# Gate and value products of five dense feed-forward stages with the weights as the stationary operand

## The chip, the core and the metric

The kernel runs as one launch on one core of a Trainium2 chip. The metric is the time on the device in microseconds (us); lower is better. The engines go by their names in the profile: PE is TensorE (its weight loads stand apart, as PEld), DVE is VectorE, ACT is ScalarE, POOL is GpSimd, SP is the engine that issues most transfers.

## What is computed

The reference runs 256 tokens of width 1024 through two blocks of two layers each: mixers (convolution and state space, dilated attention, then retention, gated recurrence and windowed attention) with feed-forward parts between them. Five of these parts are dense, with an inner width of 2816, and the change is about them:

```python
def rms_norm(x, g):
    y = xf * lax.rsqrt(jnp.mean(xf * xf, axis=-1, keepdims=True) + NORM_EPS)
    return (y * g.astype(jnp.float32)).astype(x.dtype)

def swiglu(u, w1, w2):
    gate, up = jnp.split(u @ w1, 2, axis=-1)
    return (jax.nn.silu(gate) * up) @ w2

# first block, in each of two layers, before and after the mixer:
h = h + 0.5 * rms_norm(swiglu(rms_norm(h, g[0]), ffn_w1[i, 0], ffn_w2[i, 0]), g[1])

# second block, layer 0:
ff = (jax.nn.silu(h @ w_gate) * (h @ w_up)) @ w_down
```

In order of time they are called ffn00, ffn01, ffn10, ffn11 (first block) and ff0 (second block). The last feed-forward part, of the second block's layer 1, is a mixture of experts and has code of its own, which the change leaves alone.

## The kernel before, in words

**Three products for one.** A matrix product in float32 is made of three products of a shorter format (float32r in the code, `fp32r` in the profile). Each operand is split into a high part (ACT writes it by a copy) and a low part (DVE subtracts the high part from the original). `products` (L1009) and `turned_products` (L540) issue high by high, high by low and low by high into one bank. In `products` the tokens are the stationary operand, which PEld loads, and 512 columns of weights stream past; in `turned_products` 128 columns of weights are stationary and 256 tokens stream, and the result comes out with the tokens along the free axis. The mixers use both forms, the dense stages only `products`.

**A dense stage** has 11 blocks of 256 inner columns. For each block SP loads 2 MB of gate and value weights and 1 MB of down weights. A block is split as three units: unit 0 (the first four of eight 128-row chunks of the gate and value weights), unit 1 (the other four) and unit 2 (the down weights). `pe_dense` (L1021) has this step:

- `up` of block j+1: for unit 0, then unit 1, for both halves t of the tokens, 4 chunks of 3 products of 512 columns (256 of the gate, 256 of the value) into bank 4 + t: 48 products.
- `down` of block j for the first half of the tokens: 12 products of 512 columns into the banks 0 and 1.
- `turn` of block j+1: four 128x128 transposes of the product of silu and value, so that the inner columns come to stand on the partitions, into bank 6. It waits for `hidden_ready`.
- `down` for the second half of the tokens: 12 products into the banks 2 and 3.

The first block has no `down` ahead of it; the last `down` stands behind the loop. In `act_dense` (L1156) and `dve_dense` (L1187) a step is: split unit 0 of the block after next, silu of the gate half of banks 4 and 5 (L1169, ACT), multiply with the value half (L1199 or L1203, DVE), split unit 1, high part of the turned result (L1177, ACT), low part (L1211, DVE), split unit 2. Each engine works through its list in order.

**The norm.** For the four stages of the first block the input isn't normed: the tokens' scale (`token_scale`, one number per token) is applied behind the product, as the `scale` of the silu and the scalar of DVE's multiply, where the tokens are on the partitions. So the products can start before the sum of squares is known. ff0 has no such scale.

**The start of a stage.** `pe_turn_h` (L1242) turns the hidden state h in four parts of four transposes: parts 0 and 1 are the first half of the tokens, 2 and 3 the second. ACT (L1261) and DVE (L1272) split each into `u_high` and `u_low`. All four stand ahead of the first product on PE. The first half's h comes some 2.7 us ahead of the second half's.

**The end of a stage.** ACT copies the last down unit (L1141), then, in ffn00, ffn10, ffn11 and ff0, splits the first four pieces of the next stage's weights (L407), then loads the table with the square root (L619) and squares the result (L666); DVE follows (L1150, L416, L692, L703) and writes the new h.

## Time and profile before

| what | value |
|---|---|
| time, median of 3 runs | 3358.28 us (3352.33 to 3360.78) |
| the profiled execution: its own time, its span | 3354.18 us, 3352.3 us |
| PE busy | 3183.7 us, 95% of the span |
| DVE, ACT busy | 2259.7 us (67%), 1870.2 us (56%) |
| PE's share of the chain that ended last | 89% |
| granted clock of PE, mean | 0.975 of 2.4 GHz |

The busy time of PE is not a sum of work: a product's record lasts longer than the distance to the next one, since they are pipelined. For what a product costs, the distance from start to start is read. The granted clock has two levels, 0.50 (1.2 GHz) and 1.00 (2.4 GHz).

### The profile page before, as it was taken

How to read it: one execution, taken by the hardware profiler on the slowest of the kernel's cores; microseconds unless marked ns; L12 is line 12 of the kernel's file. 1: busy time of each engine (PE TensorE's matmuls, PEld its weight loads, DVE VectorE, ACT ScalarE, POOL GpSimd, SP SyncE). 2: the span in 40 equal slices, each digit the busy share in tenths (PEclk: the TensorE clock that was granted, in tenths of full speed). 3: DMA queues.
4: the chain of work that ended last, by engine and by line, in shares of the span. 5: the costliest groups of instructions: out<-in, count | busy, mean ns of one | idle time of the engine just before them, and what ended most of it. 6: DMA issues, size and time to landing. Idle time of an engine off the chain costs nothing.

```text
span 3352.3 us, 41787 instructions
## 1 busy us (share of the span) xinstructions
PE 3183.7 (95%) x15980; PEld 2665.0 (79%) x15980; DVE 2259.7 (67%) x2676; ACT 1870.2 (56%) x2461; POOL 14.4 (0%) x26
## 2 busy tenths in 40 slices
PE   6999989999999989999899999997999999999998
PEld 5878578788887877888688788886888888788886
DVE  4549855555445565656554647555998898898997
ACT  4441354544555445646444447463777777777775
POOL 0000000000000000000000000000000000000000
PEclk9999999999999989999899999997999999999999
DMA  8444265555436444534454344434999999999994
GB/s 271 163 157 151 75 201 170 183 191 172 132 101 208 138 176 151 186 132 152 166 195 176 139 151 151 142 122 162 350 365 353 333 366 354 333 366 354 355 355 185
DMA packets 381165, 719.10 MB, mean 215 GB/s; under 512 B 14025, under 2 KB 153743, under 8 KB 380847
## 3 DMA queue, kind: packets, MB, share of 16 engines
q1 hardware_dynamic: 376384, 707.71, 59.6%
q0 software_dynamic: 2368, 8.52, 0.7%
q8 instruction: 123, 2.02, 0.2%
q10 hardware_dynamic: 2223, 0.31, 0.1%
q14 instruction: 67, 0.55, 0.0%
HBM read 715.44 MB, written 1.05 MB: 214 GB/s over the span
## 4 chain that ended last, share of the span: by engine, by line
PE 89%; DVE 5%; ACT 4%; issue 1%; ACTq 0%; DMA 0%; DVEq 0%; SPq 0%
PE duo L1011 13%; PE duo L1012 13%; PE duo L1013 13%; PE acc L1011 8%; PE acc L1013 8%; PE acc L1012 8%; PE aux L1011 2%; PE aux L1013 2%; PE aux L1012 2%; PE duo L387 1%; PE duo L542 1%; PE duo L543 1%; PE duo L544 1%; PE aux L542 1%; PE aux L543 1%; PE aux L544 1%
## 5 line engine op out<-in xcount | busy, mean ns | idle before, releaser
L1583 DVE TENSOR_TENSOR weights_split<-w,weights_split 128x1024 fp32r<-128x1024 f32 x672 | 790.6, 1221 | 107.9 <-ACT weights_split L1562 106.8
L1562 ACT ACTIVATE weights_split<-w 128x1024 fp32r<-128x1024 f32 x672 | 677.6, 1057 | 247.6 <-PE duo L1013 168.1
L1011 PE MATMUL duo<-weights_split,u_high 128*128 128x512 f32 x1776 | 699.7, 394 | 10.7 <-issue 5.8
L1013 PE MATMUL duo<-weights_split,u_low 128*128 128x512 f32 x1776 | 694.0, 391 | 1.4 <-issue 1.4
L1012 PE MATMUL duo<-weights_split,u_high 128*128 128x512 f32 x1776 | 693.8, 391 | 0.0
L416 DVE TENSOR_TENSOR w_low<-w,w_high 128x1024 fp32r<-128x1024 f32 x304 | 368.4, 1223 | 329.6 <-ACT w_high L407 328.7
L1128 DVE TENSOR_TENSOR weights_split<-w,weights_split 128x1024 fp32r<-128x1024 f32 x320 | 377.7, 1222 | 283.8 <-ACT weights_split L1116 283.6
L407 ACT ACTIVATE w_high<-w 128x1024 fp32r<-128x1024 f32 x304 | 318.1, 1057 | 348.8 <-PE acc L1013 96.3
L1116 ACT ACTIVATE weights_split<-w 128x1024 fp32r<-128x1024 f32 x320 | 322.3, 1058 | 256.6 <-PE duo L1013 155.6
L1011 PEld LDWEIGHTS duo<-weights_split,u_high 128*128 128x128 f32 x1776 | 335.6, 189 | 81.2 <-issue 13.3
L1013 PEld LDWEIGHTS duo<-weights_split,u_low 128*128 128x128 f32 x1776 | 334.9, 189 | 70.7
L1012 PEld LDWEIGHTS duo<-weights_split,u_high 128*128 128x128 f32 x1776 | 335.3, 189 | 68.3
L1011 PE MATMUL acc<-weights_split,hidden_T_split 128*128 128x512 f32 x688 | 270.1, 393 | 1.4 <-DVE hidden_T_split L1706 1.4
L1013 PE MATMUL acc<-weights_split,hidden_T_split 128*128 128x512 f32 x688 | 268.2, 390 | 0.0
L1012 PE MATMUL acc<-weights_split,hidden_T_split 128*128 128x512 f32 x688 | 267.8, 389 | 0.0
L1011 PEld LDWEIGHTS acc<-weights_split,hidden_T_split 128*128 128x128 f32 x688 | 129.2, 188 | 27.7 <-DVE hidden_T_split L1706 1.6
L1013 PEld LDWEIGHTS acc<-weights_split,hidden_T_split 128*128 128x128 f32 x688 | 129.1, 188 | 27.1
L1012 PEld LDWEIGHTS acc<-weights_split,hidden_T_split 128*128 128x128 f32 x688 | 129.3, 188 | 26.2
L1169 ACT ACTIVATE arena<-duo,small 128x256 f32<-128x256 f32 x88 | 41.8, 475 | 142.7 <-PE duo L1013 142.7
L1199 DVE SCALAR_TENSOR_TENSOR arena<-duo,small,arena 128x256 f32<-128x256 f32 x88 | 42.3, 481 | 112.0 <-ACT arena L1169 112.0
L542 PE MATMUL duo<-u_high,w_high 128*128 128x256 f32 x400 | 113.4, 283 | 0.0
L542 PE MATMUL aux<-u_high,w_high 128*128 128x256 f32 x400 | 112.4, 281 | 0.8 <-ACT arena L579 0.8
(409 smaller groups left out, 5041.8 us busy)
## 6 DMA issues: line engine op xcount, KB each, us to landing
w<-in_ffn_w_dram SPq DMA_DIRECT2D x132, 1024.0 KB, 7.6
w<-in_moe_w_gate_dram SPq DMA_DIRECT2D x112, 1024.0 KB, 7.2
w<-in_moe_w_up_dram SPq DMA_DIRECT2D x112, 1024.0 KB, 7.2
w<-in_moe_w_down_dram SPq DMA_DIRECT2D x112, 1024.0 KB, 8.0
w<-in_w_in_dram SPq DMA_DIRECT2D x92, 1024.0 KB, 7.2
w<-in_hyb_w_in_dram SPq DMA_DIRECT2D x18, 1024.0 KB, 7.4
w<-in_ffn_w_gate_dram SPq DMA_DIRECT2D x11, 1024.0 KB, 7.6
w<-in_ffn_w_up_dram SPq DMA_DIRECT2D x11, 1024.0 KB, 10.0
```

The costliest lines, as they stand in the source:

```text
L407: act.activation(w_high[:, q % PIECES, :], w1[:, n % RING, 1024 * p:1024 * (p + 1)], ACT.Copy)\
L416: dve.tensor_tensor(w_low[:, n % RING, cut], w1[:, n % RING, cut], w_high[:, q % PIECES, :], ALU.subtract).then_inc(sem("piece_split"), 1)
L542: pe.matmul(bank_out, w_hi, x_hi, start=first, stop=False, skip_group_check=True)
L543: pe.matmul(bank_out, w_hi, x_lo, start=False, stop=False, skip_group_check=True)
L544: return pe.matmul(bank_out, w_lo, x_hi, start=False, stop=last, skip_group_check=True)
L1011: pe.matmul(bank_out, x_hi, w_hi, start=first, stop=False, skip_group_check=True)
L1012: pe.matmul(bank_out, x_hi, w_lo, start=False, stop=False, skip_group_check=True)
L1013: return pe.matmul(bank_out, x_lo, w_hi, start=False, stop=last, skip_group_check=True)
L1116: act.activation(units[:, x, 0, cut], src[:, cut], ACT.Copy).then_inc(sem(f"unit_hi{x}"), 1)
L1128: m = dve.tensor_tensor(units[:, x, 1, cut], src[:, cut], units[:, x, 0, cut], ALU.subtract)
L1562: act.activation(units[:, place, 0, cut], src[:, cut], ACT.Copy).then_inc(sem("moe_high"), 1)
L1583: m = dve.tensor_tensor(units[:, place, 1, cut], src[:, cut], units[:, place, 0, cut], ALU.subtract)
```

## The change

`up` uses `turned_products`: 128 columns of weights are stationary, and 256 tokens stream. A block's up has 96 products of 256 columns in place of 48 of 512: for c in 0, 1 (128 inner columns each), for y in 0, 1 (gate, value), 4 chunks of 3 products, into bank 4 + c. The result of silu times value already has the inner columns on the partitions, so `turn` is gone, and ACT and DVE split it from SBUF.

The tokens now lie along the free axis, so a number per token can't be an instruction's scalar. A row of the scales (`scale_row`) is made at a stage's start: DVE widens the two columns (`scale_wide`), PE turns them (`turn_scale`), ACT copies the result. DVE multiplies the gate half with it in an instruction of its own, ahead of the silu. The value half isn't scaled: its factor is carried to the stage's end, in the scale of ACT's squares (`out_rms`) and in DVE's first scaling (`out_scale`).

The first half of the first block (`first_half`) is different: its products have 128 columns of tokens, so that the first half of the tokens can be multiplied before the second is there. It has 96 products of 128 columns in place of 24 of 512, and the parts 2 and 3 of `pe_turn_h` stand behind its first 24. Some semaphores of the kernel's start are merged; their instructions stay as they were.

```diff
-        def pe_dense(key, fm_key, total, body):
+        def pe_dense(key, fm_key, total, body, scaled):
...
-                    for t in range(NT):
-                        if j < 0:
-                            pe.wait_ge(sem("fm_split"), at("fm_split", (fm_key, 2 * t + x)))
...
-                        for k in range(4):
-                            m = products(bank(4 + t), uh[:, 4 * x + k, cut], ul[:, 4 * x + k, cut],
-                                         whi[:, k, :], wlo[:, k, :], first=(x == 0 and k == 0),
-                                         last=(x == 1 and k == 3))
+                    if j < 0 and x == 0:
+                        first_half(whi, wlo)
+                        continue
+                    if j < 0:
+                        pe.wait_ge(sem("fm_split"), at("fm_split", (fm_key, 3)))
+                    for c in range(2):
+                        if x == 0:
+
+                            pe.wait_ge(sem("hidden_ready"), hid0 + 2 * j + c + 1 + 2 * body * i)
+                        if x == 1 and c == 1 and j < 0 and scaled:
+                            turn_scale()
+                        for y in range(2):
+                            cut = slice(y * 256 + c * P, y * 256 + (c + 1) * P)
+                            for k in range(4):
+                                m = turned_products(bank(4 + c)[:, y * T:(y + 1) * T], whi[:, k, cut], wlo[:, k, cut],
+                                                    uh[:, 4 * x + k, :], ul[:, 4 * x + k, :],
+                                                    first=(x == 0 and y == 0 and k == 0),
+                                                    last=(x == 1 and k == 3))
...
+            def first_half(whi, wlo):
+
+                for t in range(NT):
+                    cut = slice(t * P, (t + 1) * P)
+                    for c in range(2):
+                        if t == 0:
+                            claim(4 + c)
+                        if t == 0 and c == 1:
+                            pe_turn_h(fm_key, (2, 3))
+                        pe.wait_ge(sem("fm_split"), at("fm_split", (fm_key, 2 * t)))
+                        for y in range(2):
+                            cols_of = slice(y * 256 + c * P, y * 256 + (c + 1) * P)
+                            for k in range(4):
+                                m = turned_products(bank(4 + c)[:, y * T + t * P:y * T + (t + 1) * P],
+                                                    whi[:, k, cols_of], wlo[:, k, cols_of], uh[:, k, cut],
+                                                    ul[:, k, cut], first=(t == 0 and y == 0 and k == 0), last=False)
+                m.then_inc(sem("unit_used0"), 1)
...
+            def turn_scale():
+
+                claim(6)
+                pe.wait_ge(sem("token_scale"), at("token_scale", (key, "wide")))
+                for t in range(NT):
+                    m = pe.transpose(bank(6)[:, t * P:(t + 1) * P], scale_wide[:, t, :], cst("ident"))
+                m.then_inc(bank_full(6), fill(6, (key, "scale")))
...
             def step(i, j):
                 up(i, j)
                 if j >= 0:
-                    down(i, j - 1, 0, first=(j == 0))
-                turn(i, j)
-                if j >= 0:
-                    down(i, j - 1, 1, first=(j == 0))
+                    for t in range(NT):
+                        down(i, j - 1, t, first=(j == 0))
...
+                if scaled:
+                    for c in range(2):
+                        dve.wait_ge(bank_full(4 + c), full0[c] + 2 + j + body * i)
+                        dve.tensor_tensor(silu[:, c, :], bank(4 + c)[:, 0:T], scale_row[:, :], ALU.mult)\
+                           .then_inc(sem("gate_scaled"), 1)
...
+                for c in range(2):
+                    dve.wait_ge(sem("silu_ready"), silu0 + 2 * (1 + j) + c + 1 + 2 * body * i)
+                    dve.tensor_tensor(hid[:, c, :], silu[:, c, :], bank(4 + c)[:, T:2 * T], ALU.mult)\
+                       .then_inc(sem("hidden_ready"), 1)
...
-                act.wait_ge(bank_full(6), full0[2] + 2 + j + body * i)
-                act.activation(hidden_at(j)[:, 0, :, :], split(bank(6), 2), ACT.Copy).then_inc(sem("hidT_high"), 1)
+                act.wait_ge(sem("hidden_ready"), hid0 + 2 * (j + 2) + 2 * body * i)
+                act.activation(hidden_at(j)[:, 0, :, :], hid[:, :, :], ACT.Copy).then_inc(sem("hidT_high"), 1)
```

PE's order at the start of the first dense stage (ffn00), before. L1249 are the transposes of `pe_turn_h`, `aux` the banks 6 and 7, `acc` the banks 0 and 1, `duo` the banks 4 and 5; what each waits for stands in brackets.

```order
L1249 MATMUL aux<-con,h 128x128 [waits par,h_ready]
L1249 MATMUL aux<-con,h 128x128 [waits h_ready]
L1249 MATMUL acc<-con,h 128x128 [waits h_ready]
...
L1011 MATMUL duo<-weights_split,u_high 128x512 [waits fm_split,unit_split0]
L1012 MATMUL duo<-weights_split,u_high 128x512
L1013 MATMUL duo<-weights_split,u_low 128x512
```

The same place now; L1290 are the transposes.

```order
L1290 MATMUL aux<-con,h 128x128 [waits par,h_ready]
L1290 MATMUL aux<-con,h 128x128 [waits h_ready]
L543 MATMUL duo<-u_high,weights_split 128x128 [waits fm_split,unit_split0]
L544 MATMUL duo<-u_low,weights_split 128x128
L545 MATMUL duo<-u_high,weights_split 128x128
...
L1290 MATMUL acc<-con,h 128x128 [waits h_ready]
...
L543 MATMUL duo<-u_high,weights_split 128x128 [waits fm_split]
...
L543 MATMUL duo<-u_high,weights_split 128x256 [waits fm_split,unit_split1]
...
L1085 MATMUL aux<-con,u 128x128 [waits token_scale,fm_split]
```

The second half's transposes have moved behind 24 products of 128 columns, and the two of `turn_scale` (L1085) stand inside the first block's second half.

DVE's order from one block's value products to the next in a scaled stage (ffn00, inside the loop), before. L1128 splits weights, L1199 is the multiply behind the silu, L1211 the low part of the turned result.

```order
L1128 TENSOR_TENSOR weights_split<-w,weights_split 128x1024 [waits unit_hi0]
L1199 SCALAR_TENSOR_TENSOR arena<-duo,small,arena 128x256 [waits silu_ready] x2
L1128 TENSOR_TENSOR weights_split<-w,weights_split 128x1024 [waits unit_hi1] x2
L1211 TENSOR_TENSOR hidden_T_odd<-aux,hidden_T_odd 128x512 [waits hidT_high]
L1128 TENSOR_TENSOR weights_split<-w,weights_split 128x1024 [waits unit_hi2] x2
```

And now; L1237 is the new scaling of the gate, L1243 the multiply.

```order
L1154 TENSOR_TENSOR weights_split<-w,weights_split 128x1024 [waits unit_hi0]
L1237 TENSOR_TENSOR arena<-duo,u 128x256 [waits bank_full4]
L1237 TENSOR_TENSOR arena<-duo,u 128x256 [waits bank_full5]
L1243 TENSOR_TENSOR arena<-arena,duo 128x256 [waits silu_ready] x2
L1154 TENSOR_TENSOR weights_split<-w,weights_split 128x1024 [waits unit_hi1] x2
L1251 TENSOR_TENSOR hidden_T_odd<-arena,hidden_T_odd 128x512 [waits hidT_high]
L1154 TENSOR_TENSOR weights_split<-w,weights_split 128x1024 [waits unit_hi2] x2
```

DVE scales both gate parts before it multiplies the first value part, so the first multiply stands behind a wait for bank 5.

## Rows read from the trace of the kernel before

**Rows 1.** The page, part 4: the chain that ended last, by engine.

```profile
PE 89%; DVE 5%; ACT 4%; issue 1%; ACTq 0%; DMA 0%; DVEq 0%; SPq 0%
```

**Rows 2.** Window over ffn10: length, busy of PE, PEld, DVE, ACT, POOL; PE's clock, DMA.

```profile
650.00:828.00 178.00, 176.79 (x801) 146.16 (x802) 94.03 (x112) 84.92 (x112) 0.53 (x1) 1.00 0.56 181
```

**Rows 3.** Timeline, PE in a steady block: start, length in us; first and 47th up product.

```profile
1067.23 0.39 PE L1011 MATMUL duo<-weights_split,u_high 128*128 128x512 f32 x1
...
1077.65 0.39 PE L1012 MATMUL duo<-weights_split,u_high 128*128 128x512 f32 x1
```

**Rows 4.** Timeline around the turn of that step; twelve products follow it.

```profile
1063.81 0.39 PE L1013 MATMUL acc<-weights_split,hidden_T_odd 128*128 128x512 f32 x1
...
1064.40 0.47 PE L1011 MATMUL acc<-weights_split,hidden_T_odd 128*128 128x512 f32 x1
```

**Rows 5.** Timeline, products of 256 columns in a mixer; first and 43rd.

```profile
952.35 0.28 PE L543 MATMUL aux<-u_low,w_high 128*128 128x256 f32 x1
...
957.27 0.28 PE L1012 MATMUL aux<-w_low,u_high 128*128 128x256 f32 x1
```

**Rows 6.** Timeline, float32 records of 64 and 128 columns, and what follows each.

```profile
928.38 1.45 PE L2334 MATMUL duo<-arena 128*128 128x64 f32 x12
...
929.64 0.47 PE L1011 MATMUL aux<-w_high,u_high 128*128 128x512 f32 x1
...
1431.94 3.73 PE L2756 MATMUL acc<-arena 128*128 128x128 f32 x32
...
1435.43 0.48 PE L1011 MATMUL aux<-w_high,u_high 128*128 128x512 f32 x1
```

**Rows 7.** Timeline, start of ffn10.

```profile
649.89 2.15 DVE L1272 SCALAR_TENSOR_TENSOR u_low<-aux,par,u_high 128x128 fp32r<-128x128 f32 x8
...
650.03 1.09 PE L1249 MATMUL acc<-con,h 128*128 128x128 f32 x8 [1.63 <-DVE h L703]
...
651.12 0.47 PE L1011 MATMUL duo<-weights_split,u_high 128*128 128x512 f32 x1
```

**Rows 8.** Timeline, start of ffn01, where the clock is low.

```profile
457.82 2.16 DVE L1272 SCALAR_TENSOR_TENSOR u_low<-aux,par,u_high 128x128 fp32r<-128x128 f32 x8
...
459.58 0.78 PE L1011 MATMUL duo<-weights_split,u_high 128*128 128x512 f32 x1
```

**Rows 9.** Timeline, end of the first block's up and its turn, in ffn11.

```profile
1031.57 0.39 PE L1013 MATMUL duo<-weights_split,u_low 128*128 128x512 f32 x1
...
1032.50 0.48 DVE L1199 SCALAR_TENSOR_TENSOR arena<-duo,small,arena 128x256 f32<-128x256 f32 x1 [0.90 <-ACT arena L1169]
...
1033.52 0.47 PE L1011 MATMUL duo<-weights_split,u_high 128*128 128x512 f32 x1
```

**Rows 10.** Timeline, the same place in ff0, which has no scale.

```profile
1676.98 0.39 PE L1013 MATMUL duo<-weights_split,u_low 128*128 128x512 f32 x1
...
1677.82 0.42 DVE L1203 TENSOR_TENSOR arena<-arena,duo 128x256 f32<-128x256 f32 x1 [1.63 <-ACT arena L1169]
...
1678.77 0.48 PE L1011 MATMUL duo<-weights_split,u_high 128*128 128x512 f32 x1
```

**Rows 11.** Timeline, end of ffn11: ACT and DVE behind the last up.

```profile
1195.86 0.47 ACT L1169 ACTIVATE arena<-duo,small 128x256 f32<-128x256 f32 x1 [2.25 <-PE duo L1013]
...
1197.32 2.36 DVE L1150 TENSOR_TENSOR weights_split<-w,weights_split 128x1024 fp32r<-128x1024 f32 x2 [0.47 <-ACT weights_split L1141]
```

**Rows 12.** Chain that ended last, the same stretch: start, length, what.

```profile
1199.71 3.90 ACT w_high L407 x4
...
1207.31 1.30 DVE h L703
```

**Rows 13.** Window over the router, whose records have 8 columns; columns as in rows 2.

```profile
2308.00:2318.00 10.00, 8.77 (x40) 8.47 (x40) 4.80 (x6) 5.29 (x9) 1.05 (x2) 0.50 0.89 346
```

**Rows 14.** Timeline, products of 256 columns at the low clock.

```profile
230.12 0.41 PE L544 MATMUL duo<-u_high,w_low 128*128 128x256 f32 x1
...
230.33 0.41 PE L542 MATMUL duo<-u_high,w_high 128*128 128x256 f32 x1
```

More of the change, by code:

```diff
@@ L661, in act_postnorm_sums @@
         def act_postnorm_sums(key, t):
+            dense = key not in ("mixA", "mixB")
+            if dense:
+                act.wait_ge(sem("token_scale"), at("token_scale", (key, "out")))
             for half in range(2):
@@ L1165, in step @@
                 if j < 0 and scaled:
-                    act.wait_ge(sem("token_scale"), at("token_scale", key))
-                for t in range(NT):
-                    act.wait_ge(bank_full(4 + t), full0[t] + 2 + j + body * i)
-                    act.activation(silu[:, t, :], bank(4 + t)[:, 0:256], ACT.Silu,
-                                   scale=token_scale[:, t:t + 1] if scaled else 1.0)\
+                    act.wait_ge(bank_full(6), filled_at(6, (key, "scale")))
+                    act.activation(scale_row[:, :], bank(6)[:, 0:T], ACT.Copy)\
+                       .then_inc(sem("scale_row"), mark("scale_row", key))
+                    was_read(6, (key, "scale"), "scale_row")
+                for c in range(2):
+                    if scaled:
+                        act.wait_ge(sem("gate_scaled"), gate0 + 2 * (1 + j) + c + 1 + 2 * body * i)
+                    else:
+                        act.wait_ge(bank_full(4 + c), full0[c] + 2 + j + body * i)
+                    act.activation(silu[:, c, :], silu[:, c, :] if scaled else bank(4 + c)[:, 0:T], ACT.Silu)\
                        .then_inc(sem("silu_ready"), 1)
@@ L1188, in dve_dense @@
             silu0, high0 = ev.base("silu_ready", key), ev.base("hidT_high", key)
+            full0 = [ev.base(f"bank_full{b}", key) for b in (4, 5)]
+            if scaled:
+                ev.start("gate_scaled", key)
             ev.start("hidden_ready", key)
             ev.start("hidT_split", key)
+            split0 = ev.base("hidT_split", key)
             def step(i, j):
@@ L1210, in step @@
                 x = hidden_at(j)
-                dve.tensor_tensor(x[:, 1, :, :], split(bank(6), 2), x[:, 0, :, :], ALU.subtract)\
+                dve.tensor_tensor(x[:, 1, :, :], hid[:, :, :], x[:, 0, :, :], ALU.subtract)\
                    .then_inc(sem("hidT_split"), 1)
@@ L1216, in dve_dense @@
             loop_blocks(dve, total, body, step)
+            if scaled:
+                ev.count["gate_scaled"] += 2 * total
             ev.count["hidden_ready"] += 2 * total
@@ L1301, in dve_dense_prenorm @@
                .then_inc(sem("token_scale"), mark("token_scale", key))
+            dve.wait_ge(sem("token_scale"), latest("token_scale"))
+            for t in range(NT):
+                m = dve.tensor_scalar(scale_wide[:, t, :], cst("ones"), token_scale[:, t:t + 1], None, ALU.mult)
+            m.then_inc(sem("token_scale"), mark("token_scale", (key, "wide")))
+            dve.tensor_scalar(out_rms[:, :], token_scale[:, :], D ** -0.5, None, ALU.mult)
+            dve.tensor_scalar(out_scale[:, :], token_scale[:, :], 0.5, None, ALU.mult)\
+               .then_inc(sem("token_scale"), mark("token_scale", (key, "out")))
             dve.wait_ge(sem("token_scale"), latest("token_scale"))
```

75 lines of the change are left out of this document (30 added, 45 removed).

## The prediction, made before the changed kernel ran

> **What bounds the kernel now.** I read the chain of waits first: 89% of it is PE [rows 1]. Then a window over one dense stage, where PE is busy for 176.8 of 178 us, while DVE is busy for 94 and ACT for 85, and the transfers use 56% [rows 2]. So in a dense stage the distance between PE's products decides, and whatever stands in PE's queue is on the path. The other engines count only where PE waits for them: at a stage's start, behind its first block, and at its end. A record's length says nothing about cost; I take the distance from start to start in the timeline.
>
> Prices, in us. A product of 512 columns: (1077.65 - 1067.23) / 46 = 0.2265 [rows 3]. A product of 256 columns in the same format, as the mixers use it: (957.27 - 952.35) / 42 = 0.1171 [rows 5]. That is more than half of 0.2265: a block's up goes from 48 x 0.2265 = 10.87 to 96 x 0.1171 = 11.24, so +0.37. The turn of a steady block: from the product ahead of it to the next up product lie 3.42 us and 13 products, 3.42 - 13 x 0.2265 = 0.475 [rows 3, 4]. These two nearly cancel: -0.1 a block.
>
> **A product of 128 columns** in this format is in no row, and 480 of them are added (96 in each of five stages). Every product has a weight load of its own, 128 columns of four bytes. The nearest rows are plain float32 records: with 64 columns 1.26 / 12 = 0.105, with 128 columns 3.49 / 32 = 0.109 [rows 6]. Twice the columns cost 4% more, so below 128 columns not the stream decides but something that each record pays, and the load is what they share. Bounds: 0.0586 below (half of 0.1171, if the loads hide), 0.218 above (a plain float32 product takes two such records). I take 0.109, the row with as many columns; 0.1171 would add 3.9 us to the sum.
>
> **The sum, term by term.**
>
> 1. First half of the first block: 96 x 0.109 = 10.46 in place of 24 x 0.2265 = 5.44, +5.03 a stage, five stages: +25.1.
> 2. Its start. The first product needs the first four of DVE's eight L1272. In ffn01 they are through at 457.82 + 1.08 = 458.90, and the product started at 459.58, behind the second half's transposes [rows 8]; in ffn10 it is 650.97 against 651.12 [rows 7]. So 0.68 and 0.15 are gained; I take ffn11 and ff0 as ffn01, and ffn00 as ffn10. In the first kind the clock is low (the first product lasts 0.78, not 0.47), and 0.68 us do half the work: 3 x 0.34 + 2 x 0.15 = 1.3. The eight transposes of the second half now stand in the stream of products, 8 x 0.109 = 0.87 a stage. ACT and DVE take about 2.5 us for the split behind them, which the next 24 products cover. Net 4.4 - 1.3 = +3.1.
> 3. Second half of the first block: 48 x 0.1171 - 24 x 0.2265 = +0.19, five times; the scale's turn, half of a turn's 0.475, four times: +1.9. Its input is there: the scale is made some 6 us after the first product, and the turn comes 13 us after it. ACT's copy, the table load and DVE's first scaling follow while the last 24 products run (2.8 us), just in time.
> 4. Behind the first block. In a scaled stage PE lost 1033.52 - (1031.57 + 0.23) = 1.72, turn included [rows 9]. Now the next product waits for the first multiply, and that stands behind DVE's scaling of the second gate part, which waits for bank 5. The handovers take 0.1 to 0.2 (silu 0.47 and both of them lie between 1031.80 and 1032.50 [rows 9]): 0.2 + 0.42 + 0.1 + 0.42 + 0.1 = 1.25, with 0.42 from the plain multiply [rows 10]. So -0.47, four times. In ff0 the first part is ready before the up ends: 1678.77 - 1677.21 = 1.56 goes, I take 1.5. Together -3.4.
> 5. The other ten blocks: 50 x 0.37 = +18.5. Turns: ten a stage, but in ffn00, ffn10 and ffn11 the last one runs beside term 6; 47 x 0.475 = -22.3. Together -3.8.
> 6. The stage's end. In ffn11 the chain leaves PE: silu at 1195.86, ACT's copy of the last unit, DVE's L1150 at 1197.32 [rows 11], then ACT's first pieces 3.90 and the new h at 1207.31 [rows 12]. The scaling of DVE now stands ahead of the second silu, 0.42 and a handover: +0.55, and about 0.1 (an estimate) for the squares' scale per token. Three stages: +2.0.
>
> Sum: 25.1 + 3.1 + 1.9 - 3.4 - 3.8 + 2.0 = +24.9. The profiled execution took 3354.2, so 3379.1; the median of the runs is 4.1 above it, and by that the changed kernel's comes out at **3383 us**, +0.7%.
>
> **Edits at nothing.** The two scalings of DVE (2 x 0.42 in each of 44 blocks) and the waits that they add: behind DVE's wait for bank 5 are queued the two multiplies, the split of unit 1 and the low part of the hidden values. By the lengths of the rows these end about 5.3 us after the up; PE runs the down (24 x 0.2265 = 5.4) and the next up's first half (5.6) before it asks for unit 1, and a whole block more before it asks for the low part. At the last block the cover is thin: the last down asks for both 5.4 us after the up. If that is missed by 0.5 us, it costs 0.5 in two stages, and nothing in those where ACT decides. The transfers of a block wait for the split of unit 1, 0.6 later in 16.7. The four small DVE instructions at a stage's start run while PE multiplies. The merged semaphores change no instruction.
>
> **Rivals.**
>
> A, *the loads hide*, the side of not slower. If the 128 columns stream at the rate of rows 5 and the load runs beside them, term 1 is 5 x (5.63 - 5.44) = +1 and the time 3359: same. It decides from a price of 0.0776 down, where the whole is 10 us. For it: in rows 5 load and stream lie side by side at 0.1171 without a loss that one sees. Against it: the 64-column records could then not cost 0.105. The Trainium skill (TensorE: Matmul & The Clock Gate, section "Back-to-back issue gap") gives about 81 ns for a product of 128 columns with its load in a long stream; by it the sum would be 13 us less, 3370. The records of 64 float32 columns stand at 105 ns and so don't bear it out for four-byte operands; no row here shows this format.
>
> B, *fewer than 256 columns are slow in this format*: if the product falls back to what plain float32 costs, 0.218, term 1 grows by 52 and the time is 3435. For it: no mixer uses fewer than 256 columns in this format, so nothing speaks against it. Against it: the program has one instruction a product, and no row shows that a format's price jumps with the columns.
>
> C, *the clock stays low*. In the router, records of 8 columns follow one another, PE is busy for 8.8 of 10 us, and the granted clock stays at 0.50, 1.2 GHz [rows 13]: busy records alone don't raise it. A product of 128 columns whose load takes 0.109 streams for half of that time. At 1.2 GHz 256 columns cost 0.21 [rows 14], and the load would too: 96 x 0.213 = 20.4 a first half against some 12 (low for about 3 us), and the second half begins slow, 1.7 more. In four stages about 41, 3424. Against it: the 64-column float32 records, with the same share, did not lower the clock, though they come 12 at a time.
>
> **How the numbers follow.** The main case 0.62, A 0.16, B 0.10, C 0.12. A measurement of this kernel can tell 0.3% from no change, about 10 us. The main case's own range is 3374 to 3392 (price 0.105 to 0.1171, term 4 and term 6 off by half). The range to hold 8 in 10 takes in the upper part of A and all of C but its end: 3362 to 3428. Slower by over 0.3% (above 3368): main nearly whole 0.60, B and C 0.22, less 0.01 for what the other terms may win: 0.81. Within: most of A, 0.13. Faster: 0.06, if A holds and the down and up groups join better than the rows show.
>
> **What would show it.** L543 to L545 with 128 columns and their distance in the five first halves: 0.109, or 0.059, or 0.218. The first half's length, about 10.5 to 13 us. The granted clock in the 15 us behind each stage's first product. The steady block: 16.8 before, 16.7 after, start to start. The pause behind the first block: 1.25 in the scaled stages, none in ff0. ACT's first pieces 0.6 later against the last up. The forecast is wrong if the five stages together don't grow by 15 to 35 us, or if the growth stands in the steady blocks and not in the first.

## The result, and the profile after

The changed kernel takes **3436.2 us**, median of 4 runs (3423.4 to 3443.9), against 3358.0 for the kernel before: ratio 1.023, 95% interval 1.020 to 1.027. The forecast was 3383, its range ended at 3428. Slower was right, the size was not: +78 us in place of +25. The profiled execution is the fastest of the four (3423.4, span 3421.5, 69.2 more than before), and the differences below are between the two profiled executions.

I cut each dense stage at three points that both kernels have: PE's first transpose of h, its first up product, and its first product of the down; what follows reaches to the next stage.

| from the first up product to the first of the down, us | ffn00 | ffn01 | ffn10 | ffn11 | ff0 | sum |
|---|---|---|---|---|---|---|
| before | 26.4 | 24.9 | 23.7 | 24.6 | 24.2 | 123.8 |
| after | 34.5 | 42.9 | 33.5 | 34.4 | 41.2 | 186.4 |

That stretch holds the two halves of the first block and the up of the second, and it takes +62.6 of the 69.2. The starts give 1.2 back, from each stage's first product of the down to its last PE takes 6.1 more in sum, and the stages' ends, the mixers and the part with experts take the other 1.7. In every stage it grew, but two stages grew by 17 and 18 us and three by 8 to 10. Two sizes of growth, with equal instructions, point at the clock. The timeline of PE in ffn01 (start, length in us, engine, line, what; one product each), at the first half's first product, at the first of the second half, and where the distance changes:

```profile
468.84 0.44 PE L543 MATMUL duo<-u_high,weights_split 128*128 128x128 f32 x1 [1.82 <-DVE u_low L1313]
...
490.97 0.52 PE L543 MATMUL duo<-u_high,weights_split 128*128 128x256 f32 x1
...
495.34 0.40 PE L545 MATMUL duo<-u_high,weights_split 128*128 128x256 f32 x1
495.56 0.30 PE L543 MATMUL duo<-u_high,weights_split 128*128 128x256 f32 x1
495.70 0.28 PE L544 MATMUL duo<-u_low,weights_split 128*128 128x256 f32 x1
```

The first half takes 490.97 - 468.84 = 22.1 us, 8 transposes included. The windows over it, in the columns of [rows 2] (length, busy of PE, PEld, DVE, ACT, POOL with counts, PE's clock, DMA share, GB/s):

```profile
475.60:490.90 15.30, 15.30 (x74) 15.30 (x73) 5.22 (x15) 5.94 (x14) 0.00 (x0) 0.50 0.44 144
490.90:495.40 4.50, 4.50 (x23) 4.50 (x23) 2.36 (x2) 2.01 (x2) 0.00 (x0) 0.50 0.00 0
495.40:497.00 1.60, 1.60 (x15) 1.60 (x15) 0.23 (x1) 0.63 (x2) 0.00 (x0) 0.94 0.00 0
```

PE is busy for 15.30 of 15.30 us, and the granted clock is 0.50 (1.2 GHz). It rises 4.6 us after the first product of 256 columns. In ff0 the same is seen (3.9 us after). In the kernel before, the clock rose 2.5 us after the first product of ffn01.

In ffn10 something else is to be seen. This stage began at 2.4 GHz before ([rows 7]: the clock stayed there). After:

```profile
675.90:677.00 1.10, 1.09 (x8) 0.86 (x8) 1.10 (x3) 0.83 (x4) 0.00 (x0) 1.00 0.00 0
677.00:679.80 2.80, 0.01 (x1) 0.02 (x1) 2.76 (x8) 2.03 (x8) 0.53 (x1) 1.00 0.01 3
679.80:684.80 5.00, 4.99 (x24) 5.00 (x24) 0.90 (x4) 0.00 (x0) 0.00 (x0) 0.51 0.32 108
684.80:686.40 1.60, 1.60 (x10) 1.60 (x10) 0.00 (x0) 0.42 (x2) 0.00 (x0) 0.50 0.00 0
686.40:694.60 8.20, 8.20 (x74) 8.20 (x73) 5.23 (x15) 6.02 (x14) 0.00 (x0) 0.98 0.21 65
```

The eight transposes that stood between the first parts of h and the first product are gone from there, so PE pauses for 2.8 us; the clock falls as the 128-column products begin, and rises behind the eight transposes that now stand in the stream (684.86 to 686.44). ffn00 and ffn11 rise 1.9 to 2.0 us behind theirs, ffn01 and ff0 don't. (In ffn00 the clock's row shows 1.00 throughout; there I go by the distances, 0.2146 and then 0.112.)

The lines that answer to the other rows of before: a steady block, first up product, first product of the down, first up product of the next block [rows 3]:

```profile
551.12 0.28 PE L543 MATMUL duo<-u_high,weights_split 128*128 128x256 f32 x1
...
562.64 0.40 PE L1016 MATMUL acc<-weights_split,hidden_T_odd 128*128 128x512 f32 x1
...
568.11 0.28 PE L543 MATMUL duo<-u_high,weights_split 128*128 128x256 f32 x1
```

96 products in 11.52 us, 0.1200 each, and 16.99 a block; before it was 16.79. The pause behind the first block in ffn01 [rows 9]:

```profile
498.90 0.28 PE L545 MATMUL duo<-u_high,weights_split 128*128 128x256 f32 x1
500.11 0.35 PE L543 MATMUL duo<-u_high,weights_split 128*128 128x256 f32 x1 [0.94 <-DVE arena L1243]
```

500.11 - 498.90 - 0.12 = 1.09, where 1.72 was; in ff0 there is none. The turn of the scale, which is new, in ffn01:

```profile
495.81 0.28 PE L545 MATMUL duo<-u_high,weights_split 128*128 128x256 f32 x1
495.93 0.38 PE L1085 MATMUL aux<-con,u 128*128 128x128 f32 x2
496.07 0.36 PE L543 MATMUL duo<-u_high,weights_split 128*128 128x256 f32 x1
496.27 0.28 PE L544 MATMUL duo<-u_low,weights_split 128*128 128x256 f32 x1
```

Its two transposes put 0.34 between 495.93 and 496.27, where one product's 0.12 would lie. The end of ffn11 [rows 11, 12], from PE's timeline (its first row) and the chain of waits (start, length, what):

```profile
1247.63 0.40 PE L1016 MATMUL acc<-weights_split,hidden_T_odd 128*128 128x512 f32 x1
```

```profile
1252.09 2.59 ACT w_high L408 x3
...
1259.88 1.30 DVE h L709
```

From the down's product that follows the last up to the new h: 12.25 us; before, 1207.31 - 1195.66 = 11.65. The other two stages of this kind, ffn00 and ffn10, took 11.62 and now take 12.23 and 12.22.

### The profile page after: what moved, and what is told of

It reads as the page before. It is cut to its first block, busy times and chain, and to the rows that moved or that the text cites. A ratio compares the mean times of both kernels' runs of the same rounds, so it can differ in the third digit from the quotient of the medians.

```text
span 3421.5 us, 47266 instructions
## 1 busy us (share of the span) xinstructions
PE 3243.4 (95%) x18648; PEld 2834.2 (83%) x18648; DVE 2287.5 (67%) x2780; ACT 1864.3 (54%) x2465; POOL 14.4 (0%) x26
## 4 chain that ended last, share of the span: by engine, by line
PE 89%; DVE 6%; ACT 4%; issue 1%; DMA 0%; ACTq 0%; DVEq 0%; SPq 0%
PE duo L543 8%; PE duo L544 8%; PE duo L545 8%; PE acc L1016 8%; PE acc L1017 8%; PE acc L1018 8%; PE duo L1016 7%; PE duo L1018 7%; PE duo L1017 7%; PE aux L1016 2%; PE aux L1018 2%; PE aux L1017 2%; PE duo L388 1%; PE aux L543 1%; PE aux L544 1%; PE aux L545 1%
## 5 line engine op out<-in xcount | busy, mean ns | idle before, releaser
L543 PE MATMUL duo<-u_high,weights_split 128*128 128x256 f32 (+1 forms) x1840 | 535.5, 291 | 20.9 <-DVE u_low L1313 17.2
L544 PE MATMUL duo<-u_low,weights_split 128*128 128x256 f32 (+1 forms) x1840 | 534.3, 290 | 0.0
L545 PE MATMUL duo<-u_high,weights_split 128*128 128x256 f32 (+1 forms) x1840 | 534.1, 290 | 0.0
L543 PEld LDWEIGHTS duo<-u_high,weights_split 128*128 128x128 f32 x1840 | 368.1, 200 | 24.9 <-issue 23.1
L544 PEld LDWEIGHTS duo<-u_low,weights_split 128*128 128x128 f32 x1840 | 368.1, 200 | 1.8
L545 PEld LDWEIGHTS duo<-u_high,weights_split 128*128 128x128 f32 x1840 | 368.0, 200 | 0.0
L1016 PE MATMUL duo<-weights_split,u_high 128*128 128x512 f32 x896 | 353.9, 395 | 7.8 <-issue 6.1
L1018 PE MATMUL duo<-weights_split,u_low 128*128 128x512 f32 x896 | 349.6, 390 | 0.0
L1017 PE MATMUL duo<-weights_split,u_high 128*128 128x512 f32 x896 | 349.5, 390 | 0.0
L1016 PEld LDWEIGHTS duo<-weights_split,u_high 128*128 128x128 f32 x896 | 168.7, 188 | 41.6 <-issue 8.2
L1018 PEld LDWEIGHTS duo<-weights_split,u_low 128*128 128x128 f32 x896 | 168.6, 188 | 35.7
L1017 PEld LDWEIGHTS duo<-weights_split,u_high 128*128 128x128 f32 x896 | 168.8, 188 | 33.8
L1016 PEld LDWEIGHTS acc<-weights_split,hidden_T_split 128*128 128x128 f32 x688 | 129.2, 188 | 27.8 <-DVE hidden_T_split L1754 1.7
## 6 DMA issues: line engine op xcount, KB each, us to landing
w<-in_ffn_w_up_dram SPq DMA_DIRECT2D x11, 1024.0 KB, 10.1
```

What stands on the lines that cost most here:

```text
L543: pe.matmul(bank_out, w_hi, x_hi, start=first, stop=False, skip_group_check=True)
L544: pe.matmul(bank_out, w_hi, x_lo, start=False, stop=False, skip_group_check=True)
L545: return pe.matmul(bank_out, w_lo, x_hi, start=False, stop=last, skip_group_check=True)
L1016: pe.matmul(bank_out, x_hi, w_hi, start=first, stop=False, skip_group_check=True)
L1017: pe.matmul(bank_out, x_hi, w_lo, start=False, stop=False, skip_group_check=True)
L1018: return pe.matmul(bank_out, x_lo, w_hi, start=False, stop=last, skip_group_check=True)
```

## The experiments

Two theories were to be told apart. *Low clock held*: a stream of 128-column products neither raises PE's clock nor keeps it from falling after a pause; the products cost 0.213 at 1.2 GHz, and the loss lasts until something else raises the clock. *Price at full clock*: the products are dear at 2.4 GHz too. A third question came from the steady blocks: why 0.1199 a product of 256 columns, and not the mixers' 0.1167?

### e1_fm256: the first half in 256 columns

```diff
-                for t in range(NT):
-                    cut = slice(t * P, (t + 1) * P)
-                    for c in range(2):
...
-                                m = turned_products(bank(4 + c)[:, y * T + t * P:y * T + (t + 1) * P], ...
+                pe_turn_h(fm_key, (2, 3))
+                pe.wait_ge(sem("fm_split"), at("fm_split", (fm_key, 2)))
+                for c in range(2):
...
+                            m = turned_products(bank(4 + c)[:, y * T:(y + 1) * T], ...
```

> The changed kernel, but the first half of the first block is multiplied for all 256 tokens at once: 48 products of 256 columns instead of 96 of 128, after all 16 transposes, waiting for the third part of the split. The first halves of the changed kernel take 90.5 us in the five stages together. Theory 'low clock held' (128-column products at 1.2 GHz cost 0.213 and do not raise the clock, products of 256 columns do): first product about 2.8 us later, then some 20 products at 0.213 and 28 at 0.120, 10.4 us a stage, so about 38 us less: profiled 3383, and the clock is up about 4 us behind the first product in every stage. Rival 'price at full clock' (96 x 0.112 in place of 48 x 0.120 is what costs, 5 us a stage, the start being 2.8 later): about 12 us less, 3410. Rival 'low clock whatever the columns' (the clock is low for a reason outside these products): the granted clock stays low for 9 to 27 us in the stages as now, and 3400 or more.

Measured: 3383.5 us (3381.5 to 3386.1), ratio to before 1.008 (1.006 to 1.010). The stretch of the table takes 26.2, 26.1, 26.9, 25.8, 24.5 us; the start ahead of it is 2.1 to 2.5 us longer than after's in each stage. The clock rises 3.0 to 5.5 us behind the first product; in ffn01:

```profile
465.50:469.20 3.70, 3.68 (x17) 3.70 (x18) 3.17 (x6) 3.70 (x6) 0.00 (x0) 0.50 1.05 397
469.20:473.00 3.80, 3.80 (x34) 3.80 (x33) 0.79 (x5) 0.30 (x2) 0.00 (x0) 0.99 0.97 319
```

So 53 of the 78 us (medians) hang on the products of 128 columns, although the starts come later, and the forecast of the first theory is met.

### e2_turns_ahead: the transposes back ahead of the first product

```diff
-                        if t == 0 and c == 1:
+                        if t == 0 and c == 0:
                             pe_turn_h(fm_key, (2, 3))
```

> The changed kernel, but the eight transposes of the second token half stand ahead of the first product again, as in the kernel before; the 96 products of 128 columns stay. Theory 'low clock held': in ffn10 the pause ahead of the first product shrinks, the clock stays at 2.4 GHz and the first half falls from 14.8 to 10.8 us; in ffn00 and ffn11, where those transposes stood in the stream and the clock rose 2 us behind them, it now stays low until the 256-column products of the second half, 7 to 8 us more each; ffn01 and ff0 as now. Sum about +8, 3430. Rival 'the transposes in the stream cost the time' : 1.6 us less in each stage and 3413. If the clock rises within a few us of the first product in all stages, the theory falls.

Measured: 3443.6 (3436.1 to 3449.2). The clock stays low through the whole first half in all five stages, and the stretch takes 40.0 to 41.4 in each. For four stages that was forecast; ffn10 I had wrong. It begins at 2.4 GHz and loses it behind three products, though the pause had shrunk to 1.9 us:

```profile
681.90:683.80 1.90, 0.05 (x1) 0.02 (x1) 1.86 (x5) 1.90 (x9) 0.00 (x0) 1.00 0.01 4
683.80:684.90 1.10, 1.09 (x10) 1.09 (x11) 1.10 (x6) 0.58 (x3) 0.53 (x1) 1.00 0.00 0
684.90:704.90 20.00, 20.00 (x96) 20.00 (x96) 5.96 (x18) 6.01 (x14) 0.00 (x0) 0.50 0.40 132
```

A pause of 1.6 us stood at the same place in the kernel before [rows 7], where 512 columns followed and the clock stayed. That does not make the narrow products the cause of the fall: two later runs go against it. In e12 a pause as long kept the clock ahead of 96 narrow products. In e11, which has the order of the kernel before, the clock fell behind the same pause (1.63) ahead of the first product of 512 columns:

```profile
651.30:652.90 1.60, 0.02 (x1) 0.00 (x0) 1.55 (x4) 1.60 (x8) 0.00 (x0) 1.00 0.02 5
652.90:654.40 1.50, 1.45 (x9) 1.45 (x9) 1.50 (x7) 0.86 (x4) 0.53 (x1) 0.59 0.00 0
```

What decides whether the clock falls at such a pause stays open. What the narrow products do is keep it low afterwards.

### e3_filler: the pause filled

```diff
             def first_half(whi, wlo):
+                claim(4)
+                for _ in range(24):
+                    pe.transpose(bank(4)[:, 0:P], cst("ident"), cst("ident"))
```

> The changed kernel with 24 filler transposes of the identity (into bank 4, overwritten later) in the pause ahead of the first product of each dense stage. Theory 'low clock held': the fillers raise the clock before or just as the products begin, and a stream of 128-column products that begins at 2.4 GHz stays there at 0.112 each; first product to first down is about 30.5 us in every stage (now 34.5, 42.9, 33.5, 34.4, 41.2), at most 1 us a stage lost to the fillers: 30 us less, profiled 3391. Rival 'the 128-column stream lowers the clock by itself': the clock falls again within the first half and the time stays at 3420 or more. Rival 'price at full clock': the clock rises but nothing is won beyond 5 us, 3417.

Measured: 3400.7 (3392.4 to 3404.1). The stretch takes 30.3 in four stages and 28.9 in ff0: equal to 0.01 us in the four. The profiled execution took 3399.8, 9 above its forecast. ffn01 (the pause with its fillers, then the whole first half):

```profile
466.90:470.20 3.30, 3.30 (x21) 3.30 (x20) 2.90 (x9) 1.29 (x5) 0.53 (x1) 0.63 1.10 362
470.20:481.80 11.60, 11.60 (x107) 11.60 (x105) 5.22 (x15) 6.44 (x15) 0.00 (x0) 1.00 0.62 216
```

The same 96 products and 8 transposes take 11.6 us in place of 22.1. A stream that begins at 2.4 GHz without a pause stays there. The sum of the stretch falls by 36.3; the fillers cost 5 (3.6 in ffn00, 1.3 in ffn01), and some 8 more lie in other parts of the program that hold no change, which these runs don't explain.

The fillers have 128 columns too, and at 1.2 GHz they stand 0.215 apart like the narrow products. In ff0 the clock was low when they and the transposes ahead of them began, and rose:

```profile
1696.20:1701.50 5.30, 5.30 (x25) 5.30 (x26) 5.12 (x8) 1.63 (x9) 0.00 (x0) 0.50 1.08 362
1701.50:1702.20 0.70, 0.70 (x8) 0.70 (x7) 0.70 (x4) 0.00 (x0) 0.15 (x1) 0.97 1.09 347
```

So the number of columns alone does not say whether a stream raises the clock. The fillers are plain float32 transposes of a constant; whether the format, the transpose or the data makes the difference was not tried.

### e5_before_128: only the narrow products, in the kernel before

```diff
-                        for k in range(4):
-                            m = products(bank(4 + t), ..., whi[:, k, :], wlo[:, k, :], ...
+                        width = P if x == 0 and j < 0 else COLS
+                        for g in range(COLS // width):
+                            of = slice(g * width, (g + 1) * width)
+                            for k in range(4):
+                                m = products(bank(4 + t)[:, of], ..., whi[:, k, of], wlo[:, k, of], ...
```

> The kernel before with one thing changed: in the first half of the first block each product of 512 columns becomes four of 128 (96 products instead of 24, the same columns, tokens stationary as before, nothing turned or moved). Theory 'low clock held': in the four stages that begin at 1.2 GHz the 96 products cost 0.213 each and the clock stays low into the second half, about 16 us more a stage; in ffn10, which begins at 2.4 GHz, 5.3 more. Sum +69, profiled 3423. Rival 'price at full clock': +5.3 in each of five stages, 3380. Rival 'the order or the layout of the change is what costs': within 5 us of the kernel before.

Measured: 3427.6 (3425.4 to 3430.9), ratio 1.021. Nothing is turned, moved or scaled here, and 70 us are lost. The stretch is 39.8 to 41.0 in all five stages, ffn10 too. The forecast had left ffn10 at 2.4 GHz. Its pause is that of the kernel before (1.62, and 1.63 in [rows 7]), six products run at 0.118, and then:

```profile
676.00:677.60 1.60, 1.00 (x8) 0.86 (x8) 1.60 (x6) 1.24 (x6) 0.53 (x1) 1.00 0.00 0
677.60:678.60 1.00, 1.00 (x8) 0.95 (x8) 1.00 (x5) 1.00 (x6) 0.00 (x0) 0.86 0.43 156
678.60:698.00 19.40, 19.40 (x91) 19.40 (x92) 4.51 (x12) 5.23 (x12) 0.00 (x0) 0.50 0.39 128
```

### e12_before_128_fill: the same, with the pauses filled

```diff
+                    fillers(16)
                     pe_turn_h((key, "pre"))
+                    if key == "ffn00":
+                        fillers(12)
...
+                    fillers(16)
                     pe_turn_h(("f", l))
+                    fillers(20)
```

> The kernel before with the products of the first half in four pieces of 128 columns (as in the run that took 3427.6, where nothing else was changed) and with filler transposes ahead of each dense stage (as in the run that took 3354.2; in ff0 20 more behind its own transposes). It measures what 480 products of 128 columns cost when the stages begin at 2.4 GHz. Theory 'low clock held': the stream stays at 2.4 GHz, each product costs 0.112, the first half 5.3 us more than with 512 columns in each of five stages, and the fillers of ff0 some 3 us: 3354 + 27 + 3 = 3384, 44 us less than without the fillers. Rival 'the 128-column stream brings the clock down or is dear by itself': 3415 or more.

Measured: 3401.2 (3393.1 to 3405.9), 17 above the forecast. The profiled execution took 3393.1 and says why: four stages stayed at 2.4 GHz and took 29.0, 29.0, 29.0 and 28.9; ffn01 began at 1.2 GHz and took 40.3. The median lies 8 above that execution, and the other three have no trace. Both kinds in one execution, 96 products each (ffn01, ffn10):

```profile
462.80:483.30 20.50, 20.50 (x98) 20.50 (x97) 5.04 (x13) 6.03 (x14) 0.00 (x0) 0.50 0.64 222
670.50:681.20 10.70, 10.70 (x96) 10.70 (x97) 5.43 (x15) 6.10 (x15) 0.00 (x0) 1.00 0.55 179
```

29.0 against 23.7 is +5.3 a stage, the price of the products at 2.4 GHz (0.1119 each); 40.3 is +16.6. So the higher price at 2.4 GHz is a real part of the loss, 26.5 us in five stages, and the low clock is the larger part of e5's 70. In ffn11 PE paused for 1.57 us ahead of its last eight transposes, and the narrow products behind them still ran at 2.4 GHz:

```profile
1041.40:1043.00 1.60, 0.03 (x2) 0.01 (x1) 1.55 (x4) 1.60 (x8) 0.00 (x0) 1.00 1.03 415
1044.00:1054.80 10.80, 10.80 (x97) 10.75 (x97) 5.51 (x15) 6.13 (x15) 0.80 (x2) 1.00 1.06 384
```

### e9_turns_twice: sixteen transposes in the stream

```diff
-                            pe_turn_h(fm_key, (2, 3))
+                            pe_turn_h(fm_key, (2, 3), repeat=2)
```

> The changed kernel with the eight transposes of the second token half issued twice (16 in a row, the same result) between the first 24 products of 128 columns and the other 72. In the changed kernel the clock rose within 2 us of these transposes in three of five stages and not in the other two (ffn01, ff0), where it stayed low until the 256-column products. Theory 'the transposes, not the 128-column products, raise the clock, and whether eight are enough is a matter of when they fall': with 16 the clock rises during or just behind them in all five stages; first product to first down about 34 to 35 us everywhere, so ffn01 and ff0 lose 7 to 8 us each and all pay 0.9 or less: profiled 3408, and the runs lie closer together than 3423 to 3444. Rival 'some stages are kept low by something else': ffn01 and ff0 stay above 40 us, 3425 or more.

Measured: 3417.5 (3415.7 to 3419.8). The stretch is 34.2 to 35.6 in all five stages: the clock rises in or behind the sixteen transposes every time. ffn01:

```profile
471.40:476.50 5.10, 5.06 (x24) 5.09 (x24) 0.93 (x4) 0.00 (x0) 0.00 (x0) 0.50 1.08 376
476.50:479.30 2.80, 2.80 (x18) 2.80 (x18) 0.00 (x0) 0.74 (x3) 0.00 (x0) 0.60 0.60 236
479.30:487.30 8.00, 8.00 (x75) 8.00 (x73) 5.24 (x15) 5.71 (x13) 0.00 (x0) 1.00 0.24 76
```

The profiled execution took 3415.7 where 3408 was forecast: the three stages that had risen before pay 1.0 to 2.1 us for the added transposes, not 0.9. Doing more work makes the kernel 19 us faster, and its four runs lie within 4.1 us, where the changed kernel's lie within 20.4. So that spread is read as the number of stages in which the clock rose behind the eight transposes, some 8 us each; this is argued, since the other three executions of it have no trace.

### e4_k_outer, e8_moved, e10_aligned: why 0.1199

```diff
-                        for y in range(2):
-                            for k in range(4):
+                        for k in range(4):
+                            for y in range(2):
```

> The changed kernel with the up products of 256 columns in another order: for each of the four input chunks the gate's and then the up's columns (three products into one half of the bank, then three into the other), as the mixers have it, in place of twelve in a row into one half. In the steady blocks such a product costs 0.1199 us, in the mixers 0.1172. Theory 'same half of the bank': the twelve in a row cost it, so the steady block falls from 16.98 to 16.72 and the kernel by 50 x 0.26 = 13 us. Rival 'where the weights lie' (the stationary operand comes from the units tile here, from the piece tiles there): 0.1199 stays, 16.98 stays, no difference beyond the run to run spread of this kernel (3423 to 3444). The first halves are untouched and the clock there stays low as now.

Measured: 3440.7 (3427.1 to 3454.1), 0.1199 over 4930 products. Its first halves are a second draw of the same kind: ffn01 rose early here (33.8), ffn10 late (43.1).

The next two start from e1. e8 exchanges two tiles, e10 leaves 32 bytes free:

```diff
+        hT_odd = sb("hidden_T_odd", [P, 2, 2, T], F32R)
         units = sb("weights_split", [P, 3, 2, 2048], F32R)
-        hT_odd = sb("hidden_T_odd", [P, 2, 2, T], F32R)
```

> The kernel with the first half in 256 columns, and the tile of the split weights moved by 4 KB in each partition (its place exchanged with hidden_T_odd); nothing else. The order of the products was no cause of 0.1199 against the mixers' 0.1167. Theory 'where the stationary weights lie': the distance of the 256-column products changes from 0.1199 (to 0.1167 at best, 50 blocks x 96 x 0.0032 = 15 us less, 3368). Rival 'the place is not it': 0.1199 and 3383 stay.

Measured: 3386.9 (3380.0 to 3388.1), 0.1199 over 5112 products.

```diff
         con = sb("con", [P, cat["pair16"][0]])
+        sb("con_pad", [P, 8])
```

> The kernel with the first half in 256 columns, with 32 bytes left free behind the constants tile, so that every tile behind it (the split weights, u_high, u_low, the hidden values) begins at a multiple of 64 bytes in its partition; until now they begin 32 bytes past one, while the mixers' w_high and w_low, ahead of the constants, are aligned. Theory 'where the stationary weights lie, by alignment': the 256-column products of the dense stages fall from 0.1199 to the mixers' 0.1167, 50 blocks x 96 x 0.0032 = 15 us less, 3368, with the mixers' own at 0.1167 as before. Rival 'alignment is not it': 0.1199 and 3383 stay.

Measured: 3388.4 (3385.6 to 3392.7), 0.1199 over 5121 products. But the mixers' products, 0.1165 to 0.1168 in every stretch of e1, spread from 0.113 to 0.118 here (mean 0.117). Their w_high stayed where it was and u_high moved by 32 bytes, so how the operands lie to one another seems to matter a little. The next run, e11, has the same 32 bytes and shows the same: four of its long stretches in the mixers stand at 0.1178, where the kernel before has 0.1167. Neither the order, nor 4 KB, nor alignment to 64 bytes explains the dense stages' 0.1199. This stays open.

### e11_before_aligned, e6_before_filler, e7_fm256_fill: versions

e11 is the kernel before with the 32 bytes of e10:

> The kernel before with the same 32 bytes left free. Its dense stages and the last FF stream the split weights in 512 columns at 0.2265 and keep u and the hidden values stationary; all three lie 32 bytes past a multiple of 64. Theory 'a stationary operand that is not aligned costs 0.003 a product': hidden under the 512 columns, so the median stays within 3 us of 3358; if it shows, at most 0.0032 for each of some 8500 such products, 27 us less. Rival 'alignment is not it': no difference.

Measured: 3361.1 (3359.2 to 3362.8, 11 runs), ratio 1.0008 (0.9999 to 1.0017): no difference in time, and 0.227 a product of 512 columns in both.

e6 is the kernel before with the fillers of e12, without those behind ff0's transposes:

> The kernel before with filler transposes of the identity into bank 4 while PE waits for the normalised h ahead of each dense stage (16, and 12 more ahead of the very first product). Theory 'the first products at 1.2 GHz are a loss that filling the pause takes back': in the kernel before four stages begin at 1.2 GHz, for 5.7, 2.6, 1.9 and 1.4 us; at 2.4 GHz each would be half as long, 2.8 + 1.3 + 0.9 + 0.7 = 5.8, and the transposes of h halve too (0.8 each): up to 8 us less, 3350. Rival 'the pause is needed': the fillers end after h is ready and delay the start by up to 1 us a stage: no difference. Rival 'the clock falls again in the short waits between fillers and products': no difference either, with the granted clock at 0.5 in the first products.

Measured: 3354.2 (3345.4 to 3359.7, 11 runs), ratio 0.9996 (0.9987 to 1.0005): no difference that can be measured. In the profiled execution, the fastest, four stages begin at 2.4 GHz and the stretch is 119.1 in sum, 4.7 less than before. Why the median gains nothing is open; e12 shows that the same fillers don't hold the clock in every stage.

e7 joins e1, the order of e4 and 16 fillers:

> All that was found put together on the changed kernel: first half of the first block in 256 columns with all transposes ahead, 16 filler transposes in the pause before it, and the up products in the order of e4. From the run with 256 columns alone (3383.5): its first products ran at 1.2 GHz for 3.1 to 5.5 us in each of the five stages; theory 'low clock held' gives half of that back, 10 us: 3373 if the order of the products does nothing, 3360 if it brings the mixers' 0.1172. Rival: the fillers delay the start as much as they win, 3383.

Measured: 3377.1 (3372.6 to 3382.0), ratio 1.005 (1.004 to 1.007). All five stages begin at 2.4 GHz, with 24.5 in four and 23.1 in ff0, but the wait for both token halves is still there. It is the best form of the change, and slower than the kernel before; no form of the change beat that kernel.

## Why the prediction was wrong

**The step that failed is the weight of rival C.** It named the mechanism, a first half at 1.2 GHz, and gave it 0.12. The sum priced all 480 products of term 1 at 0.109, as for a high clock, and put the low clock at nothing, though term 2 says that three stages begin low as ffn01 does. The argument against it was that float32 records of 64 columns, 12 at a time, had not lowered the clock in the mixers. That was no evidence: they stand between products of 512 columns, and here 96 narrow ones stand in a row, behind a pause. The evidence for it lay in [rows 8, 13]: four stages begin low, and a busy PE had not raised the clock in the router. e5 shows it alone: narrow products in the old kernel, +70 us. In the changed kernel the low clock costs 36 us (e3).

**C's size a stage was about right** (10.1 beyond a case that had the clock low for 3 us), but not where it applies. It left ffn10 alone, and took the other four in full. In the changed kernel it applies in full in ffn01 and ff0 (42.9 against 30.3 with fillers, 41.2 against 28.9: +12.6, +12.3) and in part in the other three (+3.3 to +4.2). Together 36.3 us, the difference of the stretch to e3; some 5 of them the kernel before lost as well (below). The profiled execution is the fastest; e2, where all five stages are low throughout, takes 203.8 in the stretch and 3444.

**B's time is near the measured one, for a reason that isn't B's.** At 0.112 the price at 2.4 GHz is nowhere near 0.218. A time that fits is not a mechanism shown.

**Term 1 was right at the high clock**: 0.1119 against 0.109, +5.3 a stage in e12 against +5.03. That rules out A too. The Trainium skill's 81 ns for 128 columns with their load (TensorE: Matmul & The Clock Gate, section "Back-to-back issue gap") isn't borne out for four-byte operands: e3, e9 and e12 all have 112 ns.

**Term 2** was counted as time gained at the start and 0.87 for transposes in the stream. The start moved by -1.2 in sum, against -1.3. At 1.2 GHz the transposes take 1.58. The term did not say that taking work out of a pause lengthens it: in ffn10 from 1.63 to 2.80 us. The clock fell there, but a longer pause is not shown to be the reason, since e2 (1.87) and e5 (1.62) lost it too.

**Terms 3 and 4** hold: the scale's turn takes 0.22 us, where 0.24 was taken; and the pause is 1.09 against 1.25, none in ff0.

**Term 5 had the wrong sign.** The price of 256 columns was carried over from the mixers (0.1171) and is 0.1199 here. (0.1199 - 0.1171) x 96 x 50 = 13.4 us: the steady block is 16.98, not 16.7. From the first product of the down to the last the stages grew by 6.1 in sum, where -5.7 was forecast (term 5 without the five ups of the second block). The 45 ups that lie there are 12.1 dearer by this price, which is nearly all of it.

**Term 6** holds: +0.60, +0.61 and +0.60 against +0.65.

With fillers (e3) the stretch is 26.3 longer than before, where the terms give 29.9. That likeness is in part luck, because the kernel before was itself low at four starts. At 2.4 GHz its stretch takes 23.7 in ffn10; with 23.7 in the other three of the first block, as e6 has them, and an estimated 23.6 in ff0 (28.9 in e12 less 5.3) it would be 118.4, not 123.8. Like for like e3 is 31.7 longer, 1.8 more than the terms, and term 5's price on the 144 products of 256 columns in each stretch is 2.0 of that. So the sum was right within 2 us for a clock that stays high.

The miss of 44 us in the profiled execution is then 33 in the stretch (36 lost to the clock, less 5 that the kernel before lost too, and 2 from the price of 256 columns) and 12 in the other blocks, again from that price.

## What to carry to other kernels

Before cutting a product's columns, look at the granted clock where the narrow products would run. Here 128 columns in place of 512 cost 5 us for 96 products at 2.4 GHz and 17 at 1.2 GHz. In all eleven first halves that had no transposes among their products and were at 1.2 GHz (e2, e5, ffn01 of e12), the clock did not rise before the wide products. Filling the pause ahead of them with transposes took 36 us out of the stretch (e3), but the fillers of e12 left one stage of five low. Narrow products straight behind wide ones might keep the high clock; no run tried it. And take a product's price from the same tiles, not from another stage with the same shape.

## What the runs showed of the hardware that was not expected

- PE busy for 15.3 of 15.3 us with the clock at 0.50. Advice to keep TensorE continuously busy (the Trainium skill, TensorE: Matmul & The Clock Gate, section "Why this matters for your kernels") is here not enough: busy with 128 columns did not raise the clock in up to 22 us, and products of 256 columns did in 3.0 to 5.5 us (e1). Transposes of 128 float32 columns, as far apart, were followed by a rise too (e3, e9).
- A pause of about 1.6 us with eight transposes behind it can lose the 2.4 GHz and can keep it. In ffn10 the clock fell behind six narrow products in e5 (1.62) and behind three in e2 (1.87), and in e11 (1.63) ahead of any product; it stayed in the kernel before (1.63, 512 columns behind it) [rows 7] and in ffn11 of e12 (1.57, 128 columns behind it). The cause is not found.
- A product of 256 columns costs 0.1199 in the dense stages, with 0.119 to 0.120 in all stretches of 20 products or more, and 0.1167 in the mixers, whose stationary weights lie in other tiles. The cause is not found.
